# Stick-breaking suffix sums in TensorE: fp32 softplus values against a high and a low fp32r part

## The reference, cut to what matters

```python
z = jnp.einsum('bhqd,bshd->bhqs', qblk, kf) * (dh ** -0.5)
causal = kpos[None, :] < qpos[:, None]
sp = jnp.where(causal, jax.nn.softplus(z), 0.0)
after = lax.cumsum(sp, axis=3, reverse=True) - sp
a = jnp.where(causal, jnp.exp(jax.nn.log_sigmoid(z) - after), 0.0)
return jnp.einsum('bhqs,bshd->bqhd', a, vf)
```

## Time and profile before

| | |
|---|---|
| median of three runs | 2383.44 us |
| profiled execution, its own time | 2383.86 us |
| span of the profile | 2381.9 us |
| TensorE matmul busy | 2347.0 us, 99% of the span |
| VectorE busy | 1319.1 us, 55% |
| ScalarE busy | 1111.0 us, 47% |
| mean granted TensorE clock | 0.979 of full speed |

### The profile page before, as it was taken

How to read it: one execution, slowest core, us unless ns; L and a number is a source line. 1 busy time by engine, 2 the same in 40 slices (tenths; PEclk the granted TensorE clock), 3 DMA queues, 4 the chain that set the end, 5 groups by cost and what they waited for, 6 DMA issues and landing times.

```text
span 2381.9 us, 27412 instructions
## 1 busy us (share of the span) xinstructions
PE 2347.0 (99%) x11220; PEld 1926.5 (81%) x11220; DVE 1319.1 (55%) x1658; ACT 1111.0 (47%) x1411; POOL 18.1 (1%) x53
## 2 busy tenths in 40 slices
PE   8999999999999899999999999999999999999999
PEld 7888778888888578888888888788887888778887
DVE  5546355456547465456547656646546555446445
ACT  5444554445444554445444353445445544555443
POOL 0000000000000000000000000000000000000000
PEclk9999999999999689999999999999999999999999
DMA  8555346546554046546655524516554665426553
GB/s 291 176 192 170 96 146 216 186 146 230 186 194 153 34 134 216 181 146 230 194 186 168 182 66 151 168 63 206 186 186 152 220 192 161 151 91 219 195 171 117
DMA packets 212941, 401.57 MB, mean 169 GB/s; under 512 B 12368, under 2 KB 30928, under 8 KB 212688
## 3 DMA queue, kind: packets, MB, share of 16 engines
q1 hardware_dynamic: 212816, 399.83, 51.4%
HBM read 398.73 MB, written 1.05 MB: 168 GB/s over the span
## 4 chain that ended last, share of the span: by engine, by line
PE 94%; DVE 3%; ACT 2%; DMA 1%; issue 1%; SPq 0%; POOL 0%; ACTq 0%; DVEq 0%; POOLq 0%
PE ps L931 27%; PE ps L933 27%; PE ps L932 27%; PE ps L974 5%; PE ps L1060 2%; PE ps L1090 2%; DVE wl L669 1%; PE ps L1125 1%; PE ps L1114 1%; DMA raw<-in_ffn_w_in 1%; ACT wh L437 1%; PE ps L1117 0%; DMA raw<-in_swa_w_in 0%; PE ps L1126 0%; PE ps L1115 0%
## 5 line engine op out<-in xcount | busy, mean ns | idle before, releaser
L669 DVE TENSOR_TENSOR wl<-raw,wh 128x1024 fp32r<-128x1024 f32 x730 | 867.6, 1222 | 503.6 <-ACT wh L437 499.1
L437 ACT ACTIVATE wh<-raw 128x1024 fp32r<-128x1024 f32 x730 | 754.2, 1059 | 599.0 <-PE ps L933 414.6
L931 PE MATMUL ps<-wh,xh 128*128 128x512 f32 (+1 forms) x2320 | 886.6, 382 | 5.1 <-DVE xl L676 4.8
L933 PE MATMUL ps<-wh,xl 128*128 128x512 f32 (+1 forms) x2320 | 877.6, 378 | 0.0
L932 PE MATMUL ps<-wl,xh 128*128 128x512 f32 (+1 forms) x2320 | 877.5, 378 | 0.0
L931 PEld LDWEIGHTS ps<-wh,xh 128*128 128x128 f32 x2320 | 438.8, 189 | 86.1 <-DVE xl L676 6.5
L933 PEld LDWEIGHTS ps<-wh,xl 128*128 128x128 f32 x2320 | 438.4, 189 | 81.6
L932 PEld LDWEIGHTS ps<-wl,xh 128*128 128x128 f32 x2320 | 439.0, 189 | 78.2
L931 PE MATMUL ps<-wh,hth 128*128 128x512 f32 x736 | 289.3, 393 | 0.2 <-DVE htl L682 0.2
L933 PE MATMUL ps<-wh,htl 128*128 128x512 f32 x736 | 286.8, 390 | 0.0
L932 PE MATMUL ps<-wl,hth 128*128 128x512 f32 x736 | 286.5, 389 | 0.0
(11 more groups left out here) (78 smaller groups left out, 1067.4 us busy)
## 6 DMA issues: line engine op xcount, KB each, us to landing
raw<-in_ffn_w_in SPq DMA_DIRECT2D x352, 512.0 KB, 4.7
raw<-in_ffn_w_out SPq DMA_DIRECT2D x176, 512.0 KB, 4.4
raw<-in_dil_w_in SPq DMA_DIRECT2D x72, 512.0 KB, 4.4
raw<-in_sb_w_in SPq DMA_DIRECT2D x48, 512.0 KB, 4.3
raw<-in_ple_w_gate SPq DMA_DIRECT2D x32, 512.0 KB, 5.0
raw<-in_sb_w_out SPq DMA_DIRECT2D x16, 512.0 KB, 3.7
gb<-in_ln_g SPq DMA_DIRECT2D x12, 512.0 KB, 4.2
gb<-in_ln_b SPq DMA_DIRECT2D x12, 512.0 KB, 5.5
```

What stands on the lines that cost most here:

```text
L437: act.activation(wh[:, u % RING, :], raw[:, u % RAWS, :], ACT.Copy).then_inc(hi_done, 1)
L669: dve.tensor_tensor(wl[:, u % RING, :], raw[:, u % RAWS, :], wh[:, u % RING, :].bitcast(F32), ALU.subtract).then_inc(lo_done, 1)
L931: pe.matmul(out_, a_h, b_h, start=start, stop=False)
L933: return pe.matmul(out_, a_l, b_h, start=False, stop=stop)
```

## The change

Two more constants, `lower` and `ones`, are copied to fp32r, by ScalarE at the start of the first mixer. VectorE's `soft` does three operations in place of one: softplus as before into `ssp`, a copy rounded to fp32r into `sph`, and the difference `ssp - sph` in fp32r into `spl`. Each waits for the one before (`own` waits for a semaphore that the operation raises when it is done), and TensorE is signalled after the third. `sph` and `spl` are views of `hth` and `htl`, buffers that the FFNs use. `cum` makes four fp32r matmuls a head in place of two fp32 ones.

```diff
+        lower_r = sb("lower_r", [P, P], F32R)
+        ones_r = sb("ones_r", [P, P], F32R)
...
+        sph, spl = (v.rearrange("p c t m -> p (c t m)").rearrange("p (b h n) -> p b h n", b=2, h=2) for v in (hth, htl))
...
+                    act.activation(lower_r[:], const("lower"), ACT.Copy).then_inc(masks_done, 1)
+                    act.activation(ones_r[:], const("ones"), ACT.Copy).then_inc(masks_done, 1)
...
                 def soft(h):
                     wait(dve, ln_done, i, hh, h)
-                    dve.scalar_tensor_tensor(ssp[:, h % 2], zpair(h), 0.0, sw[:, h % 2], ALU.max, ALU.add).then_inc(sp_done.sem, 1)
+                    own(dve.scalar_tensor_tensor(ssp[:, h % 2], zpair(h), 0.0, sw[:, h % 2], ALU.max, ALU.add))
+                    own(dve.tensor_copy(sph[:, h % 2], ssp[:, h % 2]))
+                    dve.tensor_tensor(spl[:, h % 2], ssp[:, h % 2], sph[:, h % 2].bitcast(F32), ALU.subtract).then_inc(sp_done.sem, 1)
...
                     for m in range(2):
-                        pe.matmul(zpair(h)[:, m, :], const("lower"), ssp[:, h % 2, m, :], start=False, stop=False, skip_group_check=True)
-                        ins = pe.matmul(zpair(h)[:, m, P:2 * P], const("ones"), ssp[:, h % 2, m, 2 * P:3 * P], start=False,
-                                        stop=True, skip_group_check=True)
+                        for sp_ in (sph, spl):
+                            pe.matmul(zpair(h)[:, m, :], lower_r[:], sp_[:, h % 2, m, :], start=False, stop=False, skip_group_check=True)
+                        for sp_ in (sph, spl):
+                            ins = pe.matmul(zpair(h)[:, m, P:2 * P], ones_r[:], sp_[:, h % 2, m, 2 * P:3 * P], start=False,
+                                            stop=sp_ is spl, skip_group_check=True)
...
                 if hh == 0:
-                    pe.wait_ge(masks_done, 2)
+                    pe.wait_ge(masks_done, 4)
```

## The result

| | before | changed |
|---|---|---|
| median of 20 executions | 2382.29 us | 2385.92 us |
| ratio, with its 95% interval | | 1.0018 (1.0011 to 1.0025) |
| profiled execution, its own time | 2383.86 us | 2381.31 us |
| TensorE matmul busy in the profile | 2347.0 us | 2335.7 us |
| VectorE busy in the profile | 1319.1 us | 1341.9 us |

The change costs 0.18%, some 4.3 us (interval 2.6 to 6.0). One execution of each kernel, 2596.45 and 2936.30 us, fell in a slower state; both are among the 20 of the medians, and neither enters the ratio. The forecast was 2385.0 us with a range of 2380 to 2389, but it counted from a median of 2383.44 us: it was a forecast of +1.5 us.

The account below looks back on a forecast made before the run. TensorE, holding 94% of the chain, was taken as the bound. Halves summed to +0.2 us, the clock added +1.3: +1.5 on the profiled 2383.86, which is 0.42 above the median, gave 2385.0 us; range 2380 to 2389.

Parts of the forecast that it names:

- the steps: TensorE and VectorE followed through each half of the mixers at the 16 cum steps: +0.2 us before the clock.
- The clock: Tail of layer 0's half 1: expected to fall to 1.2 GHz as well, +1.3 us on balance.
- The price of `cum`: TensorE's cum: 0.57 us a head, 1.14 a pair instead of 1.72, saving 9.3 us over 16.
- The rival with 0.22: Short fp32r matmuls in cum cost 0.22 us each, a pair 1.57; 2388.3 us at most, 2387 likelier; chance 0.12.
- VectorE's operations: VectorE after each softplus: copy 0.61 us, subtraction 0.96, two waits 0.08; signal 1.65 us later.
- the rival of a copy at 0.96: VectorE's copy to fp32r takes 0.96 us, adding 2.8 us over the halves: 2387.8 us; chance 0.06.
- Half 0: Layer 3's half 0: cum 0 waits 0.35 us, cum 3 1.5; the half keeps 0.25 us of 2.3.
- Half 1 of layer 0: av0 waits for V, cum 2 and 3 for VectorE's signal; delays overlap, cum 3 ends 1.17 us later.
- The sum: Both halves of layers 3 and 0 added before the clock: -0.25 - 0.7 + 1.17 + 0 = +0.2 us.
- The -0.7 and the 0: Half 0 of layer 0 gains about 0.7 us; half 1 of layer 3 ends within 0.1 us of before.
- The rival of a falling clock: Broken matmul work in the tails lengthens low clock, 3.4 us per 6.8 us stretch, one per layer: 2390.4 us; chance 0.18.
- What was free: ScalarE's two constant copies, some 0.3 us each, and weight splits up to 1.8 us later, covered by 2.7 us.

Follow-up runs that it names:

- the kernel with busy tails: Changed kernel plus unread matmuls (14 and 9) before TensorE's waits at cum 2 and cum 3 of half 1; 0.9999 times before.
- second run: The changed kernel run again with no edit, timed beside the kernel before; 1.0017 times before.
- Each half of the change alone: Against the kernel before: VectorE's split with cum left in fp32, 1.0027; softplus straight to fp32r with four single-pass matmuls a head, 0.9975.

## Why the prediction was right, point by point

The range and the sign held, and the steps held within about a microsecond. The clock was mis-sized: +1.3 us for one tail, where the profiles show 3.0 and 3.9 us for two. So +1.5 us was forecast and +4.3 measured. That 2385.0 lies as near as it does to 2385.92 is partly luck: the median of three that it counts from is 1.15 us above the later one of 20.

**The price of `cum`** was 1.14 us and is 1.15. The short matmuls cost 0.11 us as the transposes had said; neither the 0.067 nor the 0.22 came true, nor the 81 ns of the Trainium skill (TensorE: Matmul & The Clock Gate, Back-to-back issue gap). The rival with 0.22 was priced half a microsecond too low, besides: 3.8 on top of 2385.0 is 2388.8, not 2388.3.

**VectorE's operations** were 0.61 and 0.96 and are 0.56 and 0.96; each wait for itself cost 0.03 to 0.04. The signal comes 1.59 us later, not 1.65. The copy takes 0.56 us where the subtraction takes 0.96 for the same 768 elements, so the rival of a copy at 0.96 is closed. The Trainium skill (VectorE: DVE Perf Modes, The perf-mode tier table) has an fp32 copy within SBUF at twice the rate of a two-tensor operation, and these two durations, 1.7 to 1, go that way without showing the rate by itself.

**Half 0.** Predicted waits 0.35 and 1.5 us, measured 0.16 and 1.37. The whole half, from the first score matmul to the transposes behind it, at full clock in both kernels (layer 3 before, layer 0 changed):

```profile
2056.70 0.70 PE L1114 MATMUL ps<-arena 64*128 64x256 f32 x2
...
2087.34 1.09 PE L974 MATMUL ps<-consts,arena 128*128 128x128 f32 x8
```

```profile
236.04 0.70 PE L1121 MATMUL ps<-arena 64*128 64x256 f32 x2
...
266.20 1.09 PE L981 MATMUL ps<-consts,arena 128*128 128x128 f32 x8
```

30.64 and 30.16 us: -0.48 where -0.25 was forecast. Of four times 0.57 us, 1.8 are given back, most of it in the wait of 1.37 at cum 3, as the steps said.

**Half 1 of layer 0**, from the first score matmul to the output projection, before and changed (the latter's end is the 314.64 shown above):

```profile
287.89 0.70 PE L1114 MATMUL ps<-arena 64*128 64x256 f32 x2
...
315.22 0.50 PE L931 MATMUL ps<-wh,xh 128*128 128x512 f32 x1
```

```profile
284.88 0.70 PE L1121 MATMUL ps<-arena 64*128 64x256 f32 x2
```

27.33 and 29.76 us: +2.43, where +1.17 and, for the clock, +1.3 were forecast. The waits were forecast at 0.86 (av0), 2.4 and 1.9 us and are 0.62, 2.10 and 1.13; the last is shorter because cum 2 itself ran at half the clock. From the start of cum 3 to the output projection it is 309.94 to 314.64, 4.70 us; in the kernel with busy tails 3.06 in layer 3 (2133.91 to 2136.97). The low clock cost 1.6 us there.

The kernel with busy tails also shows the steps of half 1 alone, since its layer 0 ran this half at full clock. Its layer 0 and layer 3:

```profile
290.30 0.70 PE L1121 MATMUL ps<-arena 64*128 64x256 f32 x2
...
318.44 0.50 PE L938 MATMUL ps<-wh,xh 128*128 128x512 f32 x1
...
2107.97 0.70 PE L1121 MATMUL ps<-arena 64*128 64x256 f32 x2
...
2136.97 0.50 PE L938 MATMUL ps<-wh,xh 128*128 128x512 f32 x1
```

Layer 3 of the changed kernel, and then layers 0 and 3 of its second run:

```profile
2104.61 0.70 PE L1121 MATMUL ps<-arena 64*128 64x256 f32 x2
...
2134.16 0.50 PE L938 MATMUL ps<-wh,xh 128*128 128x512 f32 x1
```

```profile
286.52 0.70 PE L1121 MATMUL ps<-arena 64*128 64x256 f32 x2
...
316.49 0.50 PE L938 MATMUL ps<-wh,xh 128*128 128x512 f32 x1
...
2107.74 0.70 PE L1121 MATMUL ps<-arena 64*128 64x256 f32 x2
...
2138.83 0.52 PE L938 MATMUL ps<-wh,xh 128*128 128x512 f32 x1
```

All of half 1, from its first score matmul to the output projection:

| kernel and layer | us | TensorE clock |
|---|---|---|
| before, layer 0 | 27.33 | full |
| changed, tails busy, layer 0 | 28.14 | full |
| changed, layer 0 | 29.76 | 1.2 GHz in the tail |
| changed, layer 3 | 29.55 | 1.2 GHz in the tail |
| changed again, layer 0 | 29.97 | 1.2 GHz in the tail |
| changed again, layer 3 | 31.09 | 1.2 GHz in the tail, and for 3.4 us at the scores |
| changed, tails busy, layer 3 | 29.00 | 1.2 GHz for 3.4 us at the scores alone |

The steps cost half 1 +0.8 us, where +1.17 was forecast. With half 0's -0.48 that is +0.7 us for the two layers. The sum had +0.2, but the forecasts for full clock, -0.25 and +1.17 taken twice, make +1.8. The -0.7 and the 0 that were forecast for half 0 of layer 0 and half 1 of layer 3 can't be tested one by one: they took over the low-clock stretches of one profile, and those lay elsewhere in the next. So the steps were right in kind and 1.2 us too dear, and that the sum came nearer is luck.

**The clock** is the step that was mis-sized. I gave +1.3 us, for layer 0's tail alone, and left layer 3's as it was before. Measured, both tails fall, for 6.8 us each. By the table a fallen tail costs 1.6 and 1.4 us in the first profile of the changed kernel and 1.8 and 2.1 in the second, so 3.0 and 3.9 us in all. With the steps' +0.7 that makes 3.7 and 4.6 us, around the 4.3 and 4.0 that were measured; no part of the loss is left open beyond the scatter. The size for one tail was nearly right; that the second would fall too was missing. Taken off, the steps' +0.7 us is left, and the kernel with busy tails agrees (-0.2 us, interval -2.4 to +1.7).

The rival of a falling clock had the direction right, but not the price or the place. It had 3.4 us for each tail, the full price of 6.8 us at half the clock; since TensorE is idle for part of that time, the tails cost 1.4 to 2.1. And in all four tails the low clock ended before the output projection or within 0.1 us of its start. The time stayed inside the range because the range reached into that rival.

Stretches at the 64-row score matmuls come and go between executions: the kernel before had two of 6.8 us in its profile, the changed one a single one of 3.4. In both profiles the stretches in the two mixers add up to 17 us, but before 13.6 of them lay where TensorE was busy without a break. That is the likely reason why the changed kernel's profiled execution was the faster.

**What was free** stayed so: in the changed kernel's profile TensorE waits for no weight split in either mixer, and the constant copies don't show.

## What to carry to other kernels

When work moves from the busiest engine to the one behind it, follow the handover step by step: it is paid where there is nothing in front of the wait, and leaving the change out at just those steps turned 1.0017 into 0.998. Here the steps alone came out at +0.7 us, and most of the loss was the clock. Then price the clock as well, since a longer wait beside a shorter burst can slow the work after it; a few matmuls that nobody reads, put into a wait, were both the test and a cure here. Compare a small effect over many executions with their granted clocks, not over one profile of each.

## What was not expected of the hardware

Each half of the change alone lowers the mean granted clock, by 0.0011 and 0.0015; together they lower it by 0.0030. 1.7 us and 1.1 us of unread matmuls in two waits bring it back to 0.9810. In the profile of the changed kernel the clock fell at 307.3 us, 0.5 us after the end of a wait of 2.10 us; the second wait of the tail, 1.13 us, came when it was already low. TensorE had been idle no longer than that at a stretch in this half, and in layer 3 the clock fell at 2126.6, as cum 2 began behind a wait of the same 2.10 us. Beside partly idle work the low clock came cheaper than a stretch without idle time, where 6.8 us of it take 3.4: here they took 1.4 to 2.1.
